# The last expert's rows added on TensorE, and the other experts' rows read back while it runs

## The chip, the cores and the metric
The kernel runs on one core of a Trainium2 chip. The metric is the device time of one execution in microseconds (us). A core has TensorE (PE, matmuls and transposes), VectorE (DVE), ScalarE (ACT), GpSimd (POOL) and SyncE (SP, which here only issues DMAs); each runs its own instruction stream in order, and the streams meet at semaphores. SBUF is the working memory, PSUM (eight banks of 128 x 512 fp32, used here as `PS[:, bank, :]`) is where TensorE writes.

## The reference
Two transformer blocks over 512 tokens of width 1024. The first ends in a mixture of 32 experts, which is where the change is:

```
weights = p_g[:, None] * top_p          # two experts per token, each with a weight
yr = (silu(xb @ w_gate[e]) * (xb @ w_up[e])) @ w_down[e]       # per block of 128 rows
out = segment_sum(yr * row_w[:, None], row_tok)                # the two rows of a token are added
x = x + g2 * moe(h);  return rms_norm(x, final_g)              # end of block one
```

The second block starts with `h = rmsnorm(x)` and `z = h @ w_in`, a matrix of 28 weight units of 1 MB.

## The kernel before
All matmuls are done as three products of split numbers (`mm3`: high x high, high x low, low x high). So every 1 MB weight unit is loaded by SP into one of the buffers `raw[0..7]`, rounded by ACT into `whi` (`act_high`, L1206), and the rest is taken by DVE into `wlo` (`dve_low`, L1875; its event is `lo_v`). Three `whi`/`wlo` pairs form a ring. SP's loads are one list in fixed order (`LOADS`, issued by `sync_load`, L2984): a load waits until the unit that was in its `raw` buffer has been split. For the experts eight buffers rotate; from `w_in2` on, only `raw[0]` and `raw[1]` do.

An expert has six units: two for gate, two for up, two for down. `pe_experts`, `act_experts`, `dve_experts` and `pool_experts` write the order out by hand for each engine, with expert b + 1's first units interleaved with expert b's last. POOL gathers the 128 token rows of expert b + 2 with an indirect DMA (`xg`, L2849), TensorE transposes them (L847), and after the down projection ACT writes the product, scaled by the row's weight, to `yo` (L1472). POOL scatters `yo` to DRAM rows of `y_scratch` (L2841), an array of 1024 rows: one row per token and choice. Its column 1 of table `TB` has the destination row, column 0 the token, column 2 the weight; unused rows of a block have numbers out of bounds and are skipped. An overflow branch for crowded experts (`over_branch`) is skipped in these runs.

Behind the last expert (b = 31) this happens in order:
- all four engines meet (`moe_done`), and ACT waits until the scatters of experts 30 and 31 have landed;
- ACT issues eight DMAs that read `y_scratch` into `ym` (L1528), then splits the high parts of `w_in2` units 0 and 1;
- DVE takes their low parts, and adds the two choices of each group of 128 tokens (`yN`, L2349);
- TensorE transposes the sums (32 transposes, L947) into all eight banks;
- DVE adds the result to `XT` (L2352, event `x3`), ACT squares it into `yN` (L1534), and TensorE sums the squares over the partitions, once with weights `gf` and once with `ones` (L956, two times eight fp32 matmuls);
- ACT and DVE form the scale (L1537, L2356, L1539) and split the normalised rows into `HH` and `HL`, and TensorE starts on `w_in2` (L542).

## Time and profile before

| | us |
|---|---|
| three runs | 3047.74, 3054.37, 3057.34 (median 3054.37) |
| profiled execution: its own time | 3049.59 |
| its span, and mean granted TensorE clock | 3047.5, 0.971 |
| busy: TensorE | 2842.5 (93%) |
| busy: VectorE | 2259.7 (74%) |
| busy: ScalarE | 1481.1 (49%) |
| busy: GpSimd | 598.7 (20%) |

TensorE is busy for most of the span. The experts take the part from about 475 to 1068 us; the end of block one lies between 1068 and 1108 us, and everything behind it is the second block. The profiled execution is 2.1 us longer than its span, and 4.8 us under the median of the three runs.

### The profile page before, as it was taken

The numbers are of one execution on the slowest core, as the hardware profiler recorded it, in microseconds if no ns is written. First come the engines' busy times: TensorE is split into PE (matmuls) and PEld (weight loads), VectorE is DVE, ScalarE is ACT, GpSimd is POOL, SyncE is SP. The second block draws the span as 40 slices with busy tenths as digits, with TensorE's granted clock in tenths as the row PEclk, the third lists the DMA queues.
The fourth block names the chain that finished last, engine by engine and source line by source line (L and its number), as shares of the span: only waits on it lengthen the run. The fifth ranks groups of instructions, "written<-read, shape, count | busy, mean of one in ns | idle before, by whom it ended". The sixth has DMA issues, their size and how long they took to land.

```text
span 3047.5 us, 37281 instructions
## 1 busy us (share of the span) xinstructions
PE 2842.5 (93%) x13623; PEld 2366.9 (78%) x13623; DVE 2259.7 (74%) x3019; ACT 1481.1 (49%) x1990; POOL 598.7 (20%) x478
## 2 busy tenths in 40 slices
PE   5979987999999979998999989999899989999998
PEld 3657756888888748776777779999899978888887
DVE  6465547888888753887954329999998868888886
ACT  3443235888878733554542433563656623333332
POOL 0200111111111100000000010033233434444442
PEclk7999998999999989999999999999999999999999
DMA  7544636999999733232333334487779999999995
GB/s 298 170 159 156 210 114 235 373 368 369 358 358 354 261 128 122 90 115 83 108 128 132 131 114 172 164 287 289 255 280 324 356 374 358 360 370 364 358 366 185
DMA packets 203692, 746.31 MB, mean 245 GB/s; under 512 B 24816, under 2 KB 78192, under 8 KB 146416
## 3 DMA queue, kind: packets, MB, share of 16 engines
q1 hardware_dynamic: 123568, 492.93, 44.9%
q0 software_dynamic: 56912, 179.26, 16.7%
q10 hardware_dynamic: 23024, 71.67, 6.2%
q8 instruction: 111, 1.82, 0.2%
q14 instruction: 77, 0.63, 0.1%
HBM read 670.80 MB, written 98.11 MB: 252 GB/s over the span
## 4 chain that ended last, share of the span: by engine, by line
PE 51%; DVE 18%; issue 6%; DMA 5%; ACT 3%; ACTq 0%; DVEq 0%; POOL 0%; POOLq 0%
PE PS L542 44%; DVE wlo L1875 4%; DMA gbuf<-in_peer_u_dram,IDX 3%; DVE hf L2625 2%; DVE oh L2611 2%; ACT whi L1206 1%; DVE hf L2637 1%; PE PS L996 1%; PE PS L1008 1%; PE PS L847 1%; ACT HH L1845 1%; PE PS L1130 1%; DVE zo L2381 1%; DVE sS L2664 1%; DVE cand L2579 1%
## 5 line engine op out<-in xcount | busy, mean ns | idle before, releaser
L1875 DVE TENSOR_TENSOR wlo<-raw,whi 128x2048 fp32r<-128x2048 f32 x392 | 894.1, 2288 | 359.4 <-ACT whi L1206 322.8
L1206 ACT ACTIVATE whi<-raw 128x2048 fp32r<-128x2048 f32 x392 | 750.8, 1916 | 363.5 <-PE PS L542 304.5
L542 PE MATMUL PS<-HH,whi 128*128 128x512 f32 (+1 forms) x2056 | 791.4, 385 | 41.5 <-DVE wlo L1875 19.1
L542 PE MATMUL PS<-HH,wlo 128*128 128x512 f32 (+1 forms) x2056 | 755.5, 367 | 0.0
L542 PE MATMUL PS<-HL,whi 128*128 128x512 f32 (+1 forms) x2056 | 753.5, 366 | 0.0
L542 PEld LDWEIGHTS PS<-HH,whi 128*128 128x128 f32 x2056 | 393.3, 191 | 104.0 <-DVE wlo L1875 22.4
L542 PEld LDWEIGHTS PS<-HL,whi 128*128 128x128 f32 x2056 | 393.1, 191 | 46.5 <-issue 7.7
L542 PEld LDWEIGHTS PS<-HH,wlo 128*128 128x128 f32 x2056 | 391.6, 190 | 43.2
L542 PE MATMUL PS<-whi,HH 128*128 128x512 f32 (+1 forms) x896 | 352.4, 393 | 22.1 <-DVE HL L2667 16.8
L542 PE MATMUL PS<-wlo,HH 128*128 128x512 f32 (+1 forms) x896 | 348.0, 388 | 0.0
L542 PE MATMUL PS<-whi,HL 128*128 128x512 f32 (+1 forms) x896 | 347.8, 388 | 0.0
L542 PEld LDWEIGHTS PS<-whi,HH 128*128 128x128 f32 x896 | 169.9, 190 | 66.6 <-issue 29.3
L542 PE MATMUL PS<-whi,xh 128*128 128x512 f32 x512 | 208.8, 408 | 1.5 <-DVE xl L2272 1.5
L542 PE MATMUL PS<-whi,xl 128*128 128x512 f32 x512 | 203.0, 397 | 0.0
L542 PE MATMUL PS<-wlo,xh 128*128 128x512 f32 x512 | 202.8, 396 | 0.0
L542 PEld LDWEIGHTS PS<-whi,HL 128*128 128x128 f32 x896 | 170.2, 190 | 35.1 <-issue 0.7
L542 PEld LDWEIGHTS PS<-wlo,HH 128*128 128x128 f32 x896 | 170.0, 190 | 33.8
L2381 DVE SCALAR_TENSOR_TENSOR zo<-zc,cw,zo 128x512 f32<-128x512 f32 x240 | 163.9, 743 | 0.0
L2841 POOL DMA_INDIRECT y_scratch<-yo,TB x32 | 49.3, 1540 | 503.0 <-PE PS L847 438.6
L1821 ACT ACTIVATE sS<-PS 128x384 f32<-128x384 f32 x128 | 61.6, 482 | 160.1 <-PE PS L542 157.8
L2941 POOL DMA_INDIRECT gbuf<-in_peer_u_dram,IDX x64 | 101.8, 1591 | 187.3 <-DVE dots L2625 153.8
L2941 POOL DMA_INDIRECT gbuf<-in_peer_v_dram,IDX x64 | 111.4, 1741 | 124.9 <-DVE hf L2637 109.9
(415 smaller groups left out, 3912.6 us busy)
## 6 DMA issues: line engine op xcount, KB each, us to landing
raw<-in_moe_dram SPq DMA_DIRECT2D x192, 1024.0 KB, 7.3
raw<-in_u_units_dram SPq DMA_DIRECT2D x64, 1024.0 KB, 6.1
...
```

The lines of the kernel that those rows point to most:

```text
L542: ins = t.matmul(dst, a, b, start=(first and n == 0), stop=(last and n == 2))
L847: ins = t.transpose(m.PS[:, 4 + half, 128 * c:128 * c + 128], m.xg[:, i, 128 * (4 * half + c):128 * (4 * half + c) + 128], m.ident[:, :])
L996: ins = t.matmul(m.PS[:, 6, 128 * c2:T], m.vN2[:, c2, c:c + 128], m.PT[:, c2, 128 * c2:T], start=(c2 == 0), stop=(c2 == NT - 1), skip_grou ...
L1008: pe.inc(t.matmul(m.PS[:, 4 + n % 2, 0:128 * (i + 1)], m.Qa[:, h % 2, 128 * i:128 * i + 128], m.Ka[:, h % 2, 0:128 * (i + 1)], start=True, ...
L1206: a.inc(a.e.activation(m.whi[p % HRING][:, :, :], m.raw[RAW_SLOT[load_of(p)]][:, :, :], ACT.Copy), "hi", p)
L1821: a.inc(s.activation(m.sS[u % 2][:, ci, :], m.PS[:, n % 4, 0:TDN], ACT.Gelu_apprx_tanh), "act", n)
L1875: v.inc(v.e.tensor_tensor(m.wlo[h][:, :, :], m.raw[RAW_SLOT[load_of(p)]][:, :, :], m.whi[h][:, :, :].bitcast(F32), ALU.subtract), "lo_v", p)
L2381: ins = e.scalar_tensor_tensor(out=m.zo[:, k, :], in0=m.zc[:, k % 4, 2 + j:2 + j + T], scalar=m.cw[:, k, j:j + 1], in1=m.zo[:, k, :], op0= ...
L2611: v.inc(v.e.tensor_tensor(m.oh[:, n % 4, :, :, :], bass.AP(m.io128, 0, [[128, 128], [0, 2], [0, 4], [1, 128]]), bass.AP(eT, 4 * q, [[512 i ...
L2625: v.inc(e.tensor_tensor_reduce(m.jk[:, :], m.gbuf[i], m.hN[:, :], 1.0, 0.0, ALU.mult, ALU.add, m.dots[:, s:s + 1]), "dot", s)
L2841: g.dma(g.e.indirect_dma_start(m.y2[:, :], bass.IndirectOffsetOnAxis(ap=m.TB[:, b, 1:2], axis=0), m.yo[:, b % 2, :], None, bounds_check=2 ...
L2941: g.dma(g.e.indirect_dma_start(m.gbuf[i], None, m.I["peer_u"] if n < 128 else m.I["peer_v"], bass.IndirectOffsetOnAxis(ap=m.IDX[:, s:s + 1 ...
```

## The change
Expert 31's outputs no longer go to DRAM. Its rows of `y_scratch` are written with zeros by POOL after expert 0 (`pool_last_zero`: a memset of the buffer `ht`, here named `xlast`, and a scatter), and its token rows are gathered after expert 2 into the same buffer (`pool_last_rows`). SP reads `y_scratch` into `raw[6]`, `raw[7]`, `raw[2]` and `raw[3]` (four loads of 1 MB), behind the loads of `w_in2` units 0 and 1, as soon as the scatters of experts 30 and 29 have landed and the last units in those buffers have been split. DVE adds the two choices in place (`dve_sums`). ACT writes expert 31's scaled product as `yhi`, DVE the rest as `ylo`, and DVE makes `put`, a 128 x 512 matrix with a one where the row's token is the column. TensorE transposes the sums, and adds onto them in PSUM `yhi` and `ylo` times `put` for each of eight banks: 16 matmuls of 128 x 512. Banks are taken in the order 0, 1, 4, 5, 6, 7, 2, 3, since banks 2 and 3 hold expert 31's product. DVE's split of `w_in2` unit 1 goes behind the additions to `XT`.

The core of the diff:

```diff
@@ pe_turn_x
-    pe.wait_ge(o + f"xg{i}", b)
+    last = b == N_EXP - 1
+    pe.wait_ge("xlast") if last else pe.wait_ge(o + f"xg{i}", b)
...
@@ pe_experts
     for i in range(NT):
         pe.wait_ge("summed", i)
-        for kc in range(KC):
-            ins = t.transpose(m.PS[:, kc, 128 * i:128 * i + 128], m.yN[:, i, 128 * kc:128 * kc + 128], m.ident[:, :])
-            if i == NT - 1:
-                pe.inc(ins, "yturn", kc)
+    for kc in YTURN:
+        if kc in (2, 3):
+            pe.wait_ge("ylo", kc - 2)
+        for i in range(NT):
+            t.matmul(m.PS[:, kc, 128 * i:128 * i + 128], m.ym[i][:, 0, 128 * kc:128 * kc + 128], m.ident[:, :],
+                     is_transpose=True, start=(i == 0), stop=False)
+    pe.wait_ge("put")
+    pe.wait_ge("ylo", 1)
+    for kc in YTURN:
+        t.matmul(m.PS[:, kc, :], m.yhi[:, 128 * kc:128 * kc + 128], m.put[:, :], start=False, stop=False)
+        pe.inc(t.matmul(m.PS[:, kc, :], m.ylo[:, 128 * kc:128 * kc + 128], m.put[:, :], start=False, stop=True),
+               "yturn", kc)
...
@@ act_experts
-        act_outputs(a, m, b, 0, False)
+        if b + 1 < N_EXP:
+            act_outputs(a, m, b, 0, False)
...
+    for n in range(2):
+        b = N_EXP - 1
+        a.wait_ge("use_m", b, 4 + n)
+        a.inc(a.e.activation(m.yhi[:, 512 * n:512 * n + 512], m.PS[:, 2 + n, :], ACT.Copy,
+                             scale=m.TB[:, b, 2:3].bitcast(F32)), "yhi", n)
     a.mark("experts_done")
...
     a.wait_all("moe_done")
-    a.wait_ge("y_out0", N_EXP - 2)
-    a.wait_ge("y_out1", N_EXP - 1)
-    for i in range(NT):
-        for half in range(2):
-            a.dma(a.e.dma_start(m.ym[:, i, half, :], m.y2[512 * half + 128 * i:512 * half + 128 * i + 128, :]),
-                  f"ym{i}", half)
     act_high(a, m, FIRST["w_in2"] + 1)
     act_warm(a, m, ACT.Sqrt)
...
@@ dve_experts
+    last = N_EXP - 1
+    v.wait_ge("io512")
+    v.inc(e.tensor_copy(m.warm[:, :], m.TB[:, last, 0:1]), "puttok")
+    v.own()
+    v.inc(e.tensor_scalar(m.put[:, :], m.io512[:, :], m.warm[:, 0:1], None, ALU.is_equal), "put")
+    dve_sums(v, m, False)
+    for n in range(2):
+        v.wait_ge("yhi", n)
+        v.inc(e.scalar_tensor_tensor(out=m.ylo[:, 512 * n:512 * n + 512], in0=m.PS[:, 2 + n, :],
+                                     scalar=m.TB[:, last, 2:3].bitcast(F32),
+                                     in1=m.yhi[:, 512 * n:512 * n + 512].bitcast(F32), op0=ALU.mult,
+                                     op1=ALU.subtract), "ylo", n)
     v.mark("experts_done")
...
     v.wait_all("moe_done")
-    dve_low(v, m, FIRST["w_in2"] + 1)
-    for i in range(NT):
-        v.wait_ge(f"ym{i}", 1)
-        v.inc(e.tensor_tensor(m.yN[:, i, :], m.ym[:, i, 0, :], m.ym[:, i, 1, :], ALU.add), "summed", i)
-    for kc in range(KC):
+    dve_low(v, m, FIRST["w_in2"])
+    for kc in YTURN:
         v.wait_ge("yturn", kc)
         v.inc(e.scalar_tensor_tensor(out=m.XT[:, kc, :], in0=m.PS[:, kc, :], scalar=m.mod[:, 40 + kc:41 + kc],
                                      in1=m.XT[:, kc, :], op0=ALU.mult, op1=ALU.add), "x3", kc)
+    dve_low(v, m, FIRST["w_in2"] + 1)
...
@@ dve_sums (new)
+    for i in range(NT):
+        v.wait_ge(o + f"ym{i}")
+        v.inc(v.e.tensor_tensor(m.ym[i][:, 0, :], m.ym[i][:, 0, :], m.ym[i][:, 1, :], ALU.add), o + "summed", i)
...
@@ pool_last_zero, pool_last_rows (new), pool_experts
+    g.inc(g.e.memset(m.xlast, 0.0), "yzero")
+    g.own()
+    g.dma(g.e.indirect_dma_start(m.y2[:, :], bass.IndirectOffsetOnAxis(ap=m.TB[:, N_EXP - 1, 1:2], axis=0), m.xlast,
+                                 None, bounds_check=2 * T - 1, oob_is_err=False), "yzero_out")
+
+
+def pool_last_rows(g, m):
+    g.wait_ge("yzero_out")
+    g.dma(g.e.indirect_dma_start(m.xlast, None, m.h2d[:, :],
+                                 bass.IndirectOffsetOnAxis(ap=m.TB[:, N_EXP - 1, 0:1], axis=0),
+                                 bounds_check=T - 1, oob_is_err=False), "xlast")
...
-    for b in range(N_EXP):
+    for b in range(N_EXP - 1):
         pool_expert(g, m, b, False)
+        if b == 0:
+            g.wait_all("route_done")
+            g.inc(e.iota(m.io512[:, :], pattern=[[1, T]], base=0, channel_multiplier=0,
+                         allow_small_or_imprecise_dtypes=True), "io512")
+            pool_last_zero(g, m)
+        elif b == 2:
+            pool_last_rows(g, m)
...
@@ sync_program
+        if n == LOAD_OF["w_in2", 2]:
+            y.wait_ge("y_out0", N_EXP - 2)
+            y.wait_ge("y_out1", N_EXP - 3)
+            for i in range(NT):
+                y.wait_ge("lo_v", YM_AFTER[i])
+                y.dma(e.dma_start(m.ym[i], y_rows(m, i)), f"ym{i}")
```

Three places of the instruction streams, as the two programs have them. SP's queue around the first `w_in2` loads (`raw_1` is `raw[0]`, `raw_16` and `raw_17` are `raw[6]` and `raw[7]`, `raw_3` and `raw_4` are `raw[2]` and `raw[3]`), before:

```order
L2984 DMA raw_15<-in_moe_dram 128x2048
L2984 DMA raw_1<-in_w_in_dram 128x2048
L2984 DMA raw_2<-in_w_in_dram 128x2048
L2984 DMA raw_1<-in_w_in_dram 128x2048
L2984 DMA raw_2<-in_w_in_dram 128x2048
```

and now:

```order
L3058 DMA raw_15<-in_moe_dram 128x2048
L3058 DMA raw_1<-in_w_in_dram 128x2048
L3058 DMA raw_2<-in_w_in_dram 128x2048
L3091 DMA raw_16<-y_scratch 128x2x1024
L3091 DMA raw_17<-y_scratch 128x2x1024
L3091 DMA raw_3<-y_scratch 128x2x1024
L3091 DMA raw_4<-y_scratch 128x2x1024
L3058 DMA raw_1<-in_w_in_dram 128x2048
```

The four reads stand between units 1 and 2 of `w_in2`. DVE at the end of the experts, before, from the last expert's `hl` to the additions to `XT` (what is skipped belongs to the overflow branch):

```order
L2297 TENSOR_TENSOR hl<-PS,hh 128x512
L3051 TENSOR_LOAD n_over
L3052 COMPARE_AND_BRANCH
...
L1875 TENSOR_TENSOR wlo_8<-raw_1,whi_5 128x2048
L1875 TENSOR_TENSOR wlo_9<-raw_2,whi_6 128x2048
L2349 TENSOR_TENSOR yN<-ym 128x1024 x4
L2352 SCALAR_TENSOR_TENSOR XT<-PS,mod,XT 128x512 x8
L2356 RECIPROCAL ht<-ht 128x512
```

and now:

```order
L2318 TENSOR_TENSOR hl<-PS,hh 128x512
L2368 CAST warm<-TB 128x1
L2370 TENSOR_SCALAR put<-io_125,warm 128x512
L2340 TENSOR_TENSOR raw_16<-raw_16 128x1024
L2340 TENSOR_TENSOR raw_17<-raw_17 128x1024
L2340 TENSOR_TENSOR raw_3<-raw_3 128x1024
L2340 TENSOR_TENSOR raw_4<-raw_4 128x1024
L2374 SCALAR_TENSOR_TENSOR ylo<-PS,TB,yhi 128x512 x2
...
L1896 TENSOR_TENSOR wlo_8<-raw_1,whi_5 128x2048
L2391 SCALAR_TENSOR_TENSOR XT<-PS,mod,XT 128x512 x8
L1896 TENSOR_TENSOR wlo_9<-raw_2,whi_6 128x2048
```

The sums and `ylo` stand ahead of the meeting of the engines, and one of the two splits behind the additions to `XT`. POOL around experts 0 to 2, before:

```order
L2849 DMA xg<-h_scratch,TB 128x1024 x3
L2841 DMA y_scratch<-yo,TB 1024x1024
L2849 DMA xg<-h_scratch,TB 128x1024
L2841 DMA y_scratch<-yo,TB 1024x1024
L2849 DMA xg<-h_scratch,TB 128x1024
L2841 DMA y_scratch<-yo,TB 1024x1024
```

and now:

```order
L2889 DMA xg<-h_scratch,TB 128x1024 x3
L2881 DMA y_scratch<-yo,TB 1024x1024
L2930 IOTA io_125 128x512
L2909 MEMSET ht 128x1024
L2911 DMA y_scratch<-ht,TB 1024x1024
L2889 DMA xg<-h_scratch,TB 128x1024
L2881 DMA y_scratch<-yo,TB 1024x1024
L2889 DMA xg<-h_scratch,TB 128x1024
L2881 DMA y_scratch<-yo,TB 1024x1024
L2917 DMA ht<-h_scratch,TB 128x1024
```

The gather of expert 3's rows, the fourth `xg`, now stands behind an iota, a memset and the scatter of zeros.

## Rows read from the trace of the kernel before

**Rows 1.** Timeline behind the last expert: start, length (us), engine, instruction, [idle before].
```profile
1068.22 0.69 ACT L1472 ACTIVATE yo<-PS,TB 128x512 f32<-128x512 f32 x1 [2.13 <-PE PS L542]
...
1072.43 4.62 ACTq L1528 DMA_DIRECT2D ym<-y_scratch  x8
1077.10 3.71 ACT L1206 ACTIVATE whi<-raw 128x2048 fp32r<-128x2048 f32 x2 [8.19 <-issue]
...
1080.88 1.28 ACT L1238 ACT_TABLE_LOAD   x1
...
1084.82 5.66 PE L947 MATMUL PS<-ident,yN 128*128 128x128 f32 x32 [16.70 <-DVE yN L2349]
1087.93 1.22 DVE L2349 TENSOR_TENSOR yN<-ym 128x1024 f32<-128x1024 f32 x1 [0.90 <-DMA ym<-y_scratch]
1089.84 5.36 DVE L2352 SCALAR_TENSOR_TENSOR XT<-PS,mod,XT 128x512 f32<-128x512 f32 x8 [0.68 <-PE PS L947]
...
1107.61 0.47 PE L542 MATMUL PS<-HH,whi 128*128 128x512 f32 x1 [2.25 <-DVE HL L1926]
```

**Rows 2.** Chain of waits that ended last: start, length (us), what.
```profile
1060.05 8.09 PE PS L542 x24
...
1069.67 2.65 DMA y_scratch<-yo,TB
...
1073.77 7.44 DMA ym<-y_scratch
...
1091.39 13.98 PE PS L956 x32
...
1205.52 2.77 PE PS L542 x12
```

**Rows 3.** The instructions on `y_scratch` between 1045 and 1060 us, with time to landing.
```profile
L2841 POOL DMA_INDIRECT y_scratch<-yo,TB x1: 1562/1562/1562, 1051.3 to 1051.3; - x1
...
DMA to landing us min/median/max: 6.6/6.6/6.6
```

**Rows 4.** The instructions on `y_scratch` between 1000 and 1045 us.
```profile
DMA to landing us min/median/max: 8.4/8.8/9.1
```

**Rows 5.** Busy time by stretch: each engine's, then granted clock, DMA share, GB/s.
```profile
1068.00:1072.00 4.00, 0.12 (x1) 0.00 (x0) 0.00 (x0) 0.69 (x1) 0.98 (x1) 0.97 0.05 11
1072.00:1076.00 4.00, 0.00 (x0) 0.00 (x0) 0.00 (x0) 0.00 (x0) 0.00 (x0) 0.50 0.60 213
1076.00:1080.00 4.00, 0.00 (x0) 0.00 (x0) 0.86 (x1) 2.90 (x2) 0.00 (x0) 0.50 0.98 358
1080.00:1084.00 4.00, 0.00 (x0) 0.00 (x0) 4.00 (x3) 2.29 (x3) 0.00 (x0) 0.50 1.02 416
...
1086.00:1088.00 2.00, 2.00 (x11) 2.00 (x10) 1.10 (x2) 0.00 (x0) 0.00 (x0) 0.50 0.98 414
1088.00:1090.00 2.00, 2.00 (x17) 2.00 (x16) 1.32 (x2) 0.00 (x0) 0.00 (x0) 0.79 0.76 320
```

**Rows 6.** Timeline of the last DVE splits and of the last expert's `hl`.
```profile
1043.99 4.63 DVE L1875 TENSOR_TENSOR wlo<-raw,whi 128x2048 fp32r<-128x2048 f32 x2 [0.75 <-ACT whi L1206]
...
1059.21 0.69 DVE L2297 TENSOR_TENSOR hl<-PS,hh 128x512 fp32r<-128x512 f32 x1 [1.58 <-ACT hh L1463]
```

**Rows 7.** Timeline of POOL and of TensorE's transposes around experts 0 and 1.
```profile
436.47 1.80 POOL L2822 MEMSET xg<- 128x2048 f32 x1
...
509.70 1.03 POOL L2849 DMA_INDIRECT xg<-h_scratch,TB  x1 [0.30 <-issue]
...
524.17 1.04 PE L847 MATMUL PS<-ident,xg 128*128 128x128 f32 x8
```

**Rows 8.** The instructions on `xg`, whole span: time to landing.
```profile
DMA to landing us min/median/max: 3.7/8.2/11.5
```

**Rows 9.** Busy time by stretch: start of the second block.
```profile
1109.00:1112.00 3.00, 2.94 (x8) 1.69 (x9) 3.00 (x6) 1.26 (x2) 0.00 (x0) 0.56 0.00 0
...
1140.00:1160.00 20.00, 20.00 (x90) 16.57 (x89) 9.28 (x9) 8.89 (x10) 0.00 (x0) 1.00 0.34 108
```

More of the change, by code:

```diff
@@ L446, in __init__ @@
             self.yo = sb(st, "yo", [128, 2, 1024])
+            self.xlast = self.ht[:, :, :].rearrange("p a n -> p (a n)")
+            self.yhi, self.ylo = (sb(st, name, [128, 1024], F32R) for name in ("yhi", "ylo"))
+            self.io512, self.put = sb(st, "io512", [128, T]), sb(st, "put", [128, T], F32R)
             self.oraw = self.raw[RING:RING + 2]
@@ L449, in __init__ @@
         with ExitStack() as st:
-            self.ym = sb(st, "ym", [128, NT, 2, 1024])
             self.yN = sb(st, "yN", [128, 4, 1024])
         both.close()
+        self.ym = [t[:, :, :].rearrange("p (k a) n -> p k (a n)", k=2) for t in self.raw[6:8] + self.raw[2:4]]
         with ExitStack() as st:
@@ L847, in pe_turn_x @@
             ins = t.transpose(m.PS[:, 4 + half, 128 * c:128 * c + 128],
-                              m.xg[:, i, 128 * (4 * half + c):128 * (4 * half + c) + 128], m.ident[:, :])
+                              (m.xlast if last else m.xg[:, i, :])[:, 512 * half + 128 * c:512 * half + 128 * c + 128],
+                              m.ident[:, :])
         pe.inc(ins, o + "xturn", b, half)
@@ L912, in pe_overflow @@
         pe.inc(ins, "ouse_m", b, 4 + n)
+YTURN = (0, 1, 4, 5, 6, 7, 2, 3)
 def pe_experts(pe, m):
@@ L945, in pe_experts @@
         pe.wait_ge("summed", i)
-        for kc in range(KC):
-            ins = t.transpose(m.PS[:, kc, 128 * i:128 * i + 128], m.yN[:, i, 128 * kc:128 * kc + 128], m.ident[:, :])
-            if i == NT - 1:
-                pe.inc(ins, "yturn", kc)
+    for kc in YTURN:
[10 more added lines that the diff above has]
+               "yturn", kc)
     pe.wait_ge("gf")
     for r in (3, 2):
-        for kc in range(KC):
+        for n, kc in enumerate(YTURN):
             pe.wait_ge("sq", 2, kc)
@@ L956, in pe_experts @@
             pe.inc(t.matmul(m.PS[:, 3 - r, :], m.gf[:, kc, :] if r == 3 else m.ones[:, :],
-                            m.yN[:, kc // 2, 512 * (kc % 2):512 * (kc % 2) + 512], start=(kc == 0),
-                            stop=(kc == KC - 1)), "ssq", r, kc)
+                            m.yN[:, kc // 2, 512 * (kc % 2):512 * (kc % 2) + 512], start=(n == 0),
+                            stop=(n == KC - 1)), "ssq", r, n)
     pe.mark("norm_done")
@@ L1523, in act_experts @@
     a.wait_all("moe_done")
-    a.wait_ge("y_out0", N_EXP - 2)
-    a.wait_ge("y_out1", N_EXP - 1)
-    for i in range(NT):
-        for half in range(2):
-            a.dma(a.e.dma_start(m.ym[:, i, half, :], m.y2[512 * half + 128 * i:512 * half + 128 * i + 128, :]),
-                  f"ym{i}", half)
     act_high(a, m, FIRST["w_in2"] + 1)
     act_warm(a, m, ACT.Sqrt)
-    for kc in range(KC):
+    for kc in YTURN:
         a.wait_ge("x3", kc)
@@ L2311, in dve_overflow, with dve_sums @@
         next(low)
+def dve_sums(v, m, over):
+    o = "o" * over
+    for i in range(NT):
+        v.wait_ge(o + f"ym{i}")
+        v.inc(v.e.tensor_tensor(m.ym[i][:, 0, :], m.ym[i][:, 0, :], m.ym[i][:, 1, :], ALU.add), o + "summed", i)
 def dve_experts(v, m):
@@ L2342, in dve_experts @@
             dve_overflow(v, m, b)
+        dve_sums(v, m, True)
     m.last_split = N_SOLID - 1
@@ L2345, in dve_experts @@
     v.wait_all("moe_done")
-    dve_low(v, m, FIRST["w_in2"] + 1)
-    for i in range(NT):
-        v.wait_ge(f"ym{i}", 1)
-        v.inc(e.tensor_tensor(m.yN[:, i, :], m.ym[:, i, 0, :], m.ym[:, i, 1, :], ALU.add), "summed", i)
-    for kc in range(KC):
+    dve_low(v, m, FIRST["w_in2"])
+    for kc in YTURN:
         v.wait_ge("yturn", kc)
@@ L2835, in pool_expert @@
 def pool_expert(g, m, b, over):
-    o, last = "o" * over, N_BLK if over else N_EXP
+    o, last = "o" * over, N_BLK if over else N_EXP - 1
     if b + 2 < last:
@@ L2882, in pool_experts @@
         g.wait_ge("oy_out1", N_BLK - 2)
+        for i in range(NT):
+            g.dma(e.dma_start(m.ym[i], y_rows(m, i)), f"oym{i}")
         g.inc(e.memset(m.yo[:, :, 0:1], 0.0), "oclear")
@@ L2964, in pool_peer, with y_rows @@
                 pool_rows(g, m, step)
+def y_rows(m, i):
+    return bass.AP(m.y2, 128 * i * D, [[D, 128], [T * D, 2], [1, D]])
+YM_AFTER = [max(PLACE_OF[kind, i] for n, (kind, i) in enumerate(LOADS)
+                 if RAW_SLOT[n] == k and kind == "moe") for k in (6, 7, 2, 3)]
 def sync_load(y, m, n):
@@ L3011, in sync_program @@
     for n in range(1, done):
+        if n == LOAD_OF["w_in2", 2]:
+            y.wait_ge("y_out0", N_EXP - 2)
+            y.wait_ge("y_out1", N_EXP - 3)
+            for i in range(NT):
+                y.wait_ge("lo_v", YM_AFTER[i])
+                y.dma(e.dma_start(m.ym[i], y_rows(m, i)), f"ym{i}")
         sync_load(y, m, n)
@@ L3053, in over_branch @@
             q.wait_all("experts_done")
-            q.wait_ge("y_out0", N_EXP - 2)
-            q.wait_ge("y_out1", N_EXP - 1)
+            for i in range(NT):
+                q.wait_ge(f"ym{i}")
             yield
```

4 lines of the change are left out of this document (3 added, 1 removed).

## The prediction
> **What bounds the kernel now.** I read the page first: TensorE is busy 93% of the span, so time is to be had where it stands still. The timeline behind the last expert shows one such place. TensorE's last product there ends at 1068.14 us (1060.05 + 8.09) [rows 2] and its next work, the 32 transposes of the sums, starts at 1084.82, an idle time of 16.70 [rows 1]. The chain of waits names what fills it: the scatter of expert 31 lands at 1072.3 (2.65 us), then the read of `y_scratch`, whose chained piece takes 7.44, and behind it DVE's splits and sums [rows 1, 2]. Then come 5.66 us of transposes, the additions to `XT`, and 13.98 us of fp32 matmuls for the sums of squares, which end at 1105.4 [rows 1, 2]. `w_in2` starts at 1107.61 [rows 1]. The windows give the rate of the reads and TensorE's clock: the granted clock was 0.97 on average from 1068 to 1072, 0.50 (the 1.2 GHz level) from 1072 on, and rose again between 1088 and 1090, while transposes ran [rows 5].
>
> **When the sums are there now.** SP can issue the four reads when expert 30's scatter has landed: issued at 1051.3, landing 6.6 us later [rows 3], so 1057.9. The buffers are free long before: the split of the last unit in them ends with the pair at 1043.99 + 4.63 [rows 6]. How long do 4.19 MB take alone? Before, the reads started at 1072.43 [rows 1] and the windows up to 1084 moved 0.85 + 1.43 + 1.66 = 3.95 MB (rate times length) [rows 5]; the remaining 0.24 MB at 416 GB/s take 0.6 us. That is 12.2 us from the first issue. So the last read lands at 1070.2, and DVE's last sum of 1.22 us [rows 1] ends at 1071.5. Bounds: at 416 GB/s all the way behind a start of 1.5 us, 11.6 us; as it really went, beside two loads of weights, the last sum started at 1087.93, thus 15.5 us after the first issue [rows 1]. I take 12.2, since no other load runs then: units 0 and 1 are ahead of the reads in SP's queue, and unit 2 stands behind them. Unit 2 wants unit 0 split first, which will be later than the reads are issued, so it loses nothing.
>
> A page of the Trainium skill, "DMA: Bandwidth & Descriptors", section "Anatomy of one DMA — SWDGE (gpsimd) path", fits a transfer as 2.0 us plus bytes over 436 GB/s, for GpSimd's queue. By that 4.19 MB would take 11.6 us, the end would come 0.6 us earlier, and the rows of this trace, with 416 GB/s in the best window, nearly bear it out.
>
> **TensorE from 1068.1 on.** It waits for all four sums, until 1071.5, instead of 1084.8 for the first. The transposes: at the half clock 11 began in 2 us [rows 5], 0.18 each; at full clock eight take 1.04 us with a tail [rows 7], about 0.12 each. Before, the clock fell 3.9 us behind the last product [rows 2, 5], and at 1109 it was down although TensorE had begun again at 1107.61 [rows 1, 9]. I therefore take it down from 1072 to 1075.5: 22 transposes in 4 us, ten more in 1.2, end 1076.7. The sixteen new matmuls of 128 x 512 have no row; the nearest is the product of the same form, twelve in 2.77 us at full clock, 0.23 each [rows 2], so 3.7 us, end 1080.4. At the half clock all the way they would take twice as much, 7.4; below 3.7 I see no reason to go. What they need is ready: `yhi` is the old `yo` copy of 0.69 us, ended at 1068.9 [rows 1]; `ylo`, two operations like `hl` of 0.69 [rows 6], ends at 1073.0 behind the sums; banks 2 and 3 come last. `put` and its cast fall in DVE's idle time from 1059.9 [rows 6]; of them I know no duration, but anything up to some 5 us is covered, and beyond that they would delay the sums.
>
> **The chain beside it.** The engines meet when `ylo` is done, 1073.0. ACT's two splits (3.71 for both [rows 1]) give unit 0's high part at 1075.0, DVE's low part of 2.3 us (4.63 for two) [rows 6] ends at 1077.4, and the first bank is ready at 1077.2. So the additions to `XT` run 1077.4 to 1082.8 (5.36 [rows 1]). ACT's table load of 1.28 ends at 1078.4, its first square at 1079.1. TensorE is free only at 1080.4, so this chain is just covered, with 1.3 us to spare. The sums of squares then run 13.98 us [rows 2] to 1094.4, no longer fed by anything slower: before they took 0.87 per bank twice, against 0.67 per addition. The deferred split of unit 1 fits in DVE's wait for the first root, as 7 us pass from 1080.4 to there.
>
> **The sum.** 1105.4 - 1094.4 = 11.0 us. Of it 13.3 come from the earlier sums (1084.8 to 1071.5), 3.7 are spent on the new matmuls, and 1.4 come back since the old start of the squares also lay 0.9 behind the transposes and the transposes now run 0.5 shorter. What follows in the second block hangs on this point: TensorE is busy for the whole of 20 us from 1140 on [rows 9], and nothing there waits for an absolute time. So all of it should reach the end.
>
> **Earlier costs.** POOL's iota, memset and scatter of zeros delay the gather of expert 3's rows, issued at 509.70 and used by TensorE at 524.17 [rows 7]. A memset of twice the size took 1.80 us [rows 7], so 0.9; a scatter takes 1.56 [rows 3]; the iota has no row near its size, and I bound it by the larger memset, 0 to 1.8. Together with gaps that is 3 to 5 us. Landing took 8.2 at the median and 11.5 at most [rows 8]: the gather issued at 513.5 lands at 521.7, at worst at 525 to 526. I take nothing, with 2 us as the far end. The gather of expert 31's rows adds some 1.3 us in POOL's idle time, and the bytes are those of before at another time. ACT loses eight DMA issues (4.62 us [rows 1]), in a stretch where it now waits anyway.
>
> Against the profiled execution's own 3049.6 this gives 3038.6. That execution lies 4.8 under the median 3054.4 of the runs shown, which themselves spread over 9.6 us. From the median I get **3043.4 us**, 0.36% less. A change of 0.3%, 9.2 us, is about what a measurement of this kernel tells from none, so the forecast lies near that line.
>
> **Rivals.**
> - *The clock stays up, or the reads are quicker.* With a gap of only 3.4 us TensorE may not be throttled: 32 transposes in 3.8 us and the matmuls end at 1079.0; the squares then start at 1079.2 and 12.2 us are gained. With the reads at their fast bound it is 12.8. For it: 0.97 was granted from 1068 to 1072 [rows 5]. Against it: the drop at 1109 behind a shorter gap. Time 3042.
> - *The clock does not come back for the transposes.* If transposes did not count as work, all 32 would run at 0.18 (5.7 us), and eight of the matmuls at half clock as well: end 1082.5, gain 8.9, time 3045.5. Against it stands the window 1088 to 1090, in which the clock rose with nothing but transposes running [rows 5]. The Trainium skill, "TensorE: Matmul & The Clock Gate", section "Part 4: PE-mode transpose", says that full clock doesn't engage for transpose-mode; this trace disagrees, with 0.79 granted in that window. By the page this case would be the likeliest.
> - *The reads start or end late.* Expert 30's scatter lands in 8.4 to 9.1 us as in the steady state [rows 4], or the reads take the 15.5 us of before. Each us is lost in full: 1.8 to 3.3 us, gain 6 to 9, time 3047. Against it: the 6.6 us was measured under the same load of unit 1.
> - *A part is given back later*, in that the second block's start meets `w_in2` units or splits that are late, 3 to 6 us. Against: unit 2 can be loaded from 1077.4, and TensorE takes up `w_in2` at about 1096.6, with units 0 and 1 first. Time 3048.
> - *Slower: the norm runs at half clock.* If the clock once down stays down through the sparse start, 16 matmuls take 7.4 and the squares 28.0 instead of 14.0: transposes end at 1077.2, all ends at 1112.6, 7.2 us later than before, 3061.6; it decides once the granted clock is still 0.5 behind 1084. With a late gather for expert 3 on top (2 us) it reaches 0.3%. Against it: the clock came back within 5 us of steady work at 1084.8 [rows 5].
>
> **How the numbers follow.** Forecast 0.52, clock up or quick reads 0.18, transposes don't count 0.09, late reads 0.11, given back later 0.06, slower 0.04. Over 9.2 us lie about 0.46 of the forecast's share (11.0 with 1.5 for the clock's phase and 2 or 3 for the runs' own spread), 0.16 of the second and 0.04 of the third: faster 0.66. Slower by over 0.3%: 0.04 with noise. The rest, 0.30, is within. The range reaches from 3036 (14 us gained and a low median) to 3051 (late reads, a high one).
>
> **What would show it.** In the profile after: the last of the four reads lands near 1070, in the sums' wait on a DMA; TensorE idle some 3.4 us instead of 16.7 behind the last expert; 32 transposes and 16 matmuls within 9 us; granted clock 0.5 for about 3.5 us from 1072; the squares at 1080, ended at 1094.4; `w_in2` at 1096.6; TensorE not idle at 524. It is wrong if the reads land after 1073, if TensorE waits at the squares for ACT, or if the stretch from the first `w_in2` product to the end grows.

## The result, and the profile after

| | before | after |
|---|---|---|
| median of the runs of this comparison, us | 3052.68 (six runs, 3047.74 to 3059.14) | 3038.68 (six runs, 3029.92 to 3043.45) |
| ratio after to before, with 95% interval | | 0.9962 [0.9948, 0.9977] |
| profiled execution: own time; span; clock | 3049.59; 3047.5; 0.971 | 3037.57; 3035.8; 0.971 |

By the ratio the kernel is faster by 0.38%, 11.6 us of 3052.7, and the whole interval lies under 1. The two medians of the table lie 14.0 us apart, the two spans 11.7. The forecast was 11.0 us, and 3043.4 as a time. But the profile does not show the 11.0 where they were forecast. For every kernel below I cut the span in three: up to the end of TensorE's last product of expert 31, from there to the end of the sums of squares (the **piece**), and from there to the end (the **rest**). Between the two profiled executions the first part differs by 1.5 us, the piece by 8.7 (37.25 before, 28.52 after), the rest by 1.5 (1942.13 and 1940.68).

The timeline of the kernel after, behind the last expert (start, length in us, engine, instruction, idle before), answers to [rows 1]:

```profile
1056.21 2.27 SPq L3091 DMA_DIRECT2D raw<-y_scratch  x4
...
1058.68 0.49 DVE L2370 TENSOR_SCALAR put<-io,warm 128x512 fp32r<-128x512 f32 x1
...
1066.21 0.39 PE L549 MATMUL PS<-wlo,hh 128*128 128x512 f32 x1
...
1069.95 1.23 DVE L2340 TENSOR_TENSOR raw<-raw 128x1024 f32<-128x1024 f32 x1 [2.49 <-DMA raw<-y_scratch]
1071.09 1.40 DVE L2374 SCALAR_TENSOR_TENSOR ylo<-PS,TB,yhi 128x512 fp32r<-128x512 f32 x2
...
1071.32 6.43 PE L962 MATMUL PS<-ident,raw 128*128 128x128 f32 x32 [4.72 <-DVE raw L2340]
1072.58 3.71 ACT L1226 ACTIVATE whi<-raw 128x2048 fp32r<-128x2048 f32 x2 [5.20 <-DVE ylo L2374]
1074.62 2.29 DVE L1896 TENSOR_TENSOR wlo<-raw,whi 128x2048 fp32r<-128x2048 f32 x1 [2.13 <-ACT whi L1226]
...
1078.32 5.36 DVE L2391 SCALAR_TENSOR_TENSOR XT<-PS,mod,XT 128x512 f32<-128x512 f32 x8 [1.41 <-PE PS L968]
...
1079.10 5.30 ACT L1555 ACTIVATE yN<-XT 128x512 f32<-128x512 f32 x8 [1.24 <-DVE XT L2391]
...
1097.37 0.71 PE L549 MATMUL PS<-HH,whi 128*128 128x512 f32 x1 [2.24 <-DVE HL L1947]
```

Its chain of waits (start, length, what) answers to [rows 2]:

```profile
1049.73 6.46 DMA y_scratch<-yo,TB
...
1057.66 12.26 DMA raw<-y_scratch
```

The chain goes through the same kinds of work as before, but the reads are now issued while expert 31 still computes, and expert 31's own scatter is gone from it. TensorE's idle time is 4.72 us where it was 16.70. ACT's first square starts at 1079.10, 0.8 us behind the first addition, and takes 0.66 (5.30 / 8); TensorE comes to it at 1081.23 with no wait. So the meeting of the two chains is as forecast.

The windows of the kernel after, over the same stretch (columns as in [rows 5]: TensorE, its loads, DVE, ACT, POOL busy, granted clock, DMA share, GB/s):

```profile
1056.00:1058.00 2.00, 0.86 (x4) 0.46 (x4) 0.28 (x2) 0.60 (x1) 0.00 (x0) 0.62 0.31 53
1058.00:1062.00 4.00, 3.34 (x8) 2.70 (x9) 1.96 (x4) 0.00 (x0) 0.00 (x0) 0.50 1.02 416
1062.00:1066.00 4.00, 4.00 (x16) 3.16 (x16) 1.55 (x2) 0.69 (x1) 0.00 (x0) 0.84 1.04 421
1066.00:1068.00 2.00, 0.59 (x3) 0.17 (x1) 1.23 (x1) 0.69 (x1) 0.00 (x0) 1.00 0.90 358
1068.00:1070.00 2.00, 0.00 (x0) 0.00 (x0) 0.05 (x1) 0.00 (x0) 0.00 (x0) 1.00 0.11 33
1070.00:1072.00 2.00, 0.68 (x4) 0.71 (x5) 2.00 (x3) 0.00 (x0) 0.00 (x0) 0.53 0.03 8
1072.00:1074.00 2.00, 2.00 (x11) 2.00 (x11) 0.49 (x1) 1.42 (x1) 0.00 (x0) 0.50 0.04 8
1074.00:1076.00 2.00, 2.00 (x11) 2.00 (x10) 1.38 (x1) 2.00 (x2) 0.00 (x0) 0.50 0.00 0
1076.00:1078.00 2.00, 2.00 (x14) 1.96 (x13) 0.91 (x1) 1.78 (x3) 0.00 (x0) 0.76 0.16 20
```

Three things are to be read here. The data of the four reads has moved by 1068 (416 x 4 + 421 x 4 + 358 x 2 makes 4.06 of 4.19 MB, and 0.1 before 1058), at 416 to 421 GB/s; yet the last read lands at 1069.92, nearly 2 us later, with the DMA engines at a tenth. The clock is down to 1.2 GHz (0.50) from about 1070.1 to 1077.0, 6.9 us, and comes back while transposes run. And it had been down once before: from about 1056.5 on, behind a gap of only 2.39 us (TensorE stood still from 1053.77 to 1056.16, then had 0.86 us of transposes), so that the first products of expert 31's down projection ran at 1.2 GHz.

The early costs, in POOL's timeline of the kernel after:

```profile
506.42 1.58 POOL L2881 DMA_INDIRECT y_scratch<-yo,TB  x1 [27.50 <-ACT yo L1492]
508.01 0.60 POOL L2930 IOTA io<- 128x512 f32 x1
508.53 0.97 POOL L2909 MEMSET ht<- 128x1024 f32 x1
510.30 1.47 POOL L2911 DMA_INDIRECT y_scratch<-ht,TB  x1 [0.80 <-POOL ht L2909]
512.08 1.91 POOL L2889 DMA_INDIRECT xg<-h_scratch,TB  x1 [0.31 <-issue]
```

The gather of expert 3's rows is issued 5.66 us behind expert 0's scatter, where it was 1.89 before (509.70 [rows 7] behind a scatter at 507.81). TensorE transposes its rows at 522.75, 16.33 behind that scatter; before it was 524.17 - 507.81 = 16.36. Nothing is lost. Of the two gathers issued from 505 to 530 us the first is the slower one (512.08 + 9.5 = 521.6):

```profile
DMA to landing us min/median/max: 8.4/8.9/9.5
```

In the kernel before, this gather landed 5.6 us after its issue.

### The profile page after: what moved, and what is told of

It is laid out like the page before. It is cut to its first block, busy times and chain, and to the rows that moved or that the text cites. A ratio compares the mean times of both kernels' runs of the same rounds, so it can differ in the third digit from the quotient of the medians.

```text
span 3035.8 us, 37322 instructions
## 1 busy us (share of the span) xinstructions
PE 2851.3 (94%) x13639; PEld 2375.3 (78%) x13639; DVE 2261.9 (75%) x3023; ACT 1483.0 (49%) x1990; POOL 600.4 (20%) x480
## 4 chain that ended last, share of the span: by engine, by line
PE 52%; DVE 17%; issue 7%; DMA 5%; ACT 3%; ACTq 0%; DVEq 0%; POOL 0%; SPq 0%; POOLq 0%
PE PS L549 45%; DVE wlo L1896 3%; DMA gbuf<-in_peer_u_dram,IDX 3%; DVE hf L2665 2%; DVE oh L2651 2%; ACT whi L1226 1%; DVE hf L2677 1%; PE PS L1016 1%; PE PS L1028 1%; PE PS L855 1%; ACT HH L1866 1%; DMA ht<-in_peer_u_dram,IDX 1%; PE PS L1150 1%; DVE cand L2619 1%; DVE cand L2616 1%
```

## The experiments

All kernels are edits of the changed kernel. The time is the median of the runs, with their number. The last product's end, the piece and the rest are from each profiled execution's timeline (us):

| kernel | time (runs) | last product's end | idle behind it | transposes, from first to last | piece | rest |
|---|---|---|---|---|---|---|
| before | 3052.68 (6) | 1068.12 | 16.70 | 5.66 | 37.25 | 1942.13 |
| after | 3038.68 (6) | 1066.60 | 4.72 | 6.43 | 28.52 | 1940.68 |
| a0_again | 3039.58 (7) | 1068.96 | 4.74 | 6.44 | 28.57 | 1940.27 |
| a0_third | 3037.96 (5) | 1068.17 | 6.42 | 5.62 | 29.44 | 1939.99 |
| e1_late_reads | 3051.63 (12) | 1073.10 | 14.77 | 6.47 | 38.63 | 1941.17 |
| e2_splits_first | 3036.58 (1) | 1068.78 | 4.83 | 6.38 | 28.60 | 1937.42 |
| e3_fill | 3035.89 (1) | 1065.10 | filled | 3.66 | 27.31 | 1941.69 |
| e4_free_reads | 3035.74 (1) | 1071.13 | 1.77 | 3.69 | 23.35 | 1939.52 |
| e5_groups | 3038.88 (1) | 1070.81 | 1.17 | 5.71 | 25.85 | 1940.44 |
| e6_groups_ylo | 3038.69 (5) | 1070.50 | 2.71 | 5.38 | 26.16 | 1940.24 |
| e7_x3_first | 3037.22 (5) | 1068.87 | 1.40 | 4.41 | 23.21 | 1944.02 |
| e7_again | 3037.16 (6) | 1067.96 | 1.32 | 4.72 | 23.44 | 1943.40 |
| e8_four_memsets | 3043.93 (1) | 1069.63 | 4.68 | 6.53 | 28.59 | 1943.98 |

After, a0_again and a0_third are one program: its pieces lie within 0.9 us of each other and its rests within 0.7. The last product's end moves by 8 us among these executions, and nearly all of that is there before any instruction that differs: POOL's scatter of expert 0 starts between 504.72 (e3) and 512.79 (e1), and from there to the last product of expert 31 every one of the thirteen takes 560.2 to 560.4 us. So a time from one run, or one profiled span, says little about an edit; the piece does.

**The changed kernel once more, and its reads held back.** `a0_again` has no edit. `e1_late_reads` keeps all of the change but lets SP issue the four reads only when expert 31's last product is done:

```diff
             y.wait_ge("y_out1", N_EXP - 3)
+            y.wait_ge("use_m", N_EXP - 1, 5)
```

> The changed kernel once more, as it is, for the comparisons of this call. Theory A: the whole gain arises between TensorE's last product of expert 31 and its last sum of squares; that piece was 37.2 us before and 28.5 after, so here it is 28.5 again (within 0.5), and the other 3.0 us of the 11.7 us between the two spans (1.5 ahead of that piece, 1.5 behind it) are chance and change from run to run. Ratio to the kernel before 0.996 to 0.998. Rival B: the 3.0 us belong to the change; then the last product of expert 31 again ends at 1066.6 or earlier, and from the last sum of squares to the end it again takes 1940.7 or less.

> SP issues the four reads of y_scratch only when TensorE has ended expert 31's last product; the outputs of expert 31 are still added on TensorE. Theory A (the gain is the reads beside the last expert): the reads take 13.7 us from 1066.6, the last sum ends at 1081.6, and the piece from the last product to the last sum of squares is 28.5 + 10.4 = 38.9 us, 1.7 longer than the 37.2 of before: adding on TensorE by itself costs a little. Ratio to before 1.000 to 1.001. Rival C (the gain is that expert 31's scatter and its landing, 3.5 us, are gone from the chain): the piece is about 34 to 35, and the ratio 0.999.

`a0_again` took 3039.58 us (ratio 0.9967 [0.9954, 0.9979]). Its piece is 28.57 again. Of the 3.0 us outside the piece, the 1.5 ahead of it did not come again (the last product ended at 1068.96), but the rest did (1940.27, and 1939.99 in `a0_third`), so the part of the rival that concerns the rest stands; with one profile of the kernel before it can't be settled. `e1_late_reads` took 3051.63, ratio 1.0008 [0.9999, 1.0017]: without the early reads all of the gain is gone. Its timeline:

```profile
1073.21 2.40 SPq L3092 DMA_DIRECT2D raw<-y_scratch  x4
...
1086.49 1.23 DVE L2340 TENSOR_TENSOR raw<-raw 128x1024 f32<-128x1024 f32 x1 [1.20 <-DMA raw<-y_scratch]
...
1087.87 6.47 PE L962 MATMUL PS<-ident,raw 128*128 128x128 f32 x32 [14.76 <-DVE raw L2340]
```

The piece is 38.63 where 38.9 was expected, and the rival's 34 to 35 is refuted: the reads need 13.3 us from the first issue to the last landing here too (13.7 in the kernel after), so what hides them is only their early start. Beside `a0_again` the early issue is worth 10.1 us of piece and 12.0 of median. Leaving out expert 31's scatter alone buys nothing: the wait is 1.9 us shorter than before, but the transposes take 0.8 longer, and 3.5 us instead of 0.9 pass between them and the squares, most of it in the sixteen matmuls.

**TensorE kept busy through its wait.** `e3_fill` puts twenty products behind the last expert, into a bank that is written anew afterwards:

```diff
     pe.mark("moe_done")
+    for n in range(20):
+        t.matmul(m.PS[:, 0, :], m.hh[:, x, n % 4, :], m.whi[h][:, n % 4, :], start=True, stop=True)
```

> Twenty more products of 128 x 512 into bank 0 behind expert 31's last product, whose result is overwritten: TensorE has something to do while it waits for the sums. Theory A': the clock is then still at full when the transposes start; they take about 3.8 us in place of 6.43, and the piece from the last product of the expert to the last sum of squares falls from 28.5 to 26 (the additions to XT, first at 1076.9 behind the split of w_in2's unit 0, may take back up to 0.5). Rival D: the transposes take 6.4 us for another reason than the clock (their order over banks, or four different source buffers), and the piece stays at 28.5 or grows.

```profile
1066.59 4.93 PE L958 MATMUL PS<-whi,hh 128*128 128x512 f32 x20 [1.49 <-issue]
...
1068.41 1.22 DVE L2343 TENSOR_TENSOR raw<-raw 128x1024 f32<-128x1024 f32 x1 [2.28 <-DMA raw<-y_scratch]
...
1071.36 3.66 PE L965 MATMUL PS<-ident,raw 128*128 128x128 f32 x32
```

The transposes take 3.66 us instead of 6.43, so 2.8 us of the piece are the clock that fell in the wait, and the rival that they are slow for another reason is refuted. The twenty products outlast the last sum (1069.63) by 1.7 us, which is why the piece is 27.31 and not the 25.6 that it would be without them; the one run took 3035.89 us, which can't be told from the kernel after.

**The reads free of the scatters.** `e4_free_reads` reads the token rows instead of `y_scratch`, so that SP waits for no scatter (it leaves out the experts' outputs; POOL takes over the two waits behind its last expert):

```diff
-            y.wait_ge("y_out0", N_EXP - 2)
-            y.wait_ge("y_out1", N_EXP - 3)
...
-                y.dma(e.dma_start(m.ym[i], y_rows(m, i)), f"ym{i}")
+                y.dma(e.dma_start(m.ym[i], bass.AP(m.h2d, 128 * i * D, [[D, 128], [0, 2], [1, D]])), f"ym{i}")
```

> The four reads take the same bytes from another DRAM array (the token rows), so they need not wait for the scatters of experts 29 and 30; the sums are then not those of the reference. Theory A: the reads are issued at about 1050.5, land beside unit 1 of w_in2 by 1066, the sums are done before the last product, TensorE has no gap, the clock stays up, and the piece becomes bound by expert 31's own ylo and the split of w_in2's unit 0: about 22 to 23 us. Rival E: the reads end after the expert in any case, because DMA is full, and the piece stays above 27.

```profile
1055.39 2.47 SPq L3091 DMA_DIRECT2D raw<-h_scratch  x4
...
1071.52 1.23 DVE L2340 TENSOR_TENSOR raw<-raw 128x1024 f32<-128x1024 f32 x1 [1.19 <-DMA raw<-h_scratch]
...
1072.90 3.69 PE L962 MATMUL PS<-ident,raw 128*128 128x128 f32 x32 [1.77 <-DVE raw L2340]
```

The piece is 23.35, near the 22 to 23 expected, but one step of the expectation failed: the wait did not go wholly. They stand behind `w_in2` unit 1 in SP's queue, which waits for its buffer until 1055.02, so they started 15.7 us ahead of the last product's end (1071.13), where it is 10.4 in the kernel after, and with unit 1's load beside them they took 16.1. A wait of 1.77 us is left. A gap of 1.8 us did not bring the clock down for the transposes, one of 4.7 did; for what lies between see `e6_groups_ylo`.

**Both deferred splits done first.** `e2_splits_first` takes the low part of unit 1 at its old place, in front of the additions:

```diff
-    dve_low(v, m, FIRST["w_in2"])
+    dve_low(v, m, FIRST["w_in2"] + 1)
     for kc in YTURN:
```

(and no low part behind them).

> DVE takes the low part of w_in2's unit 1 ahead of the additions to XT again, as before the change. Theory A: that chain has room, since TensorE is the later one; the additions start 0.9 us later (1079.2 in the time of the first trace, in place of 1078.3), the first square is ready at 1080.7, still ahead of TensorE at 1081.2, and the piece from expert 31's last product to the last sum of squares stays at 28.5 (within 0.3). Rival F: moving the split is part of the gain; then the piece grows by the length of the split, 2.3 us, to 30.8.

```profile
1076.91 4.49 DVE L1896 TENSOR_TENSOR wlo<-raw,whi 128x2048 fp32r<-128x2048 f32 x2 [2.12 <-ACT whi L1226]
...
1081.32 5.35 DVE L2391 SCALAR_TENSOR_TENSOR XT<-PS,mod,XT 128x512 f32<-128x512 f32 x8
1082.10 5.30 ACT L1555 ACTIVATE yN<-XT 128x512 f32<-128x512 f32 x8 [1.95 <-DVE XT L2391]
...
1083.49 7.03 PE L976 MATMUL PS<-yN,gf 128*128 128x512 f32 x16
```

The first square starts at 1082.10, is ready 0.66 later, and TensorE comes at 1083.49 without a wait. The piece is 28.60 (28.5 expected, 30.8 by the rival). So the deferred split earns nothing: the side chain has 0.7 us of room even with the split ahead of it, since TensorE is later than forecast.

**Transposes by groups, in the wait.** In the changed kernel TensorE waits for all four sums, so that its transposes end 6.6 us behind the last sum (1077.75 and 1071.18); before, they ran beside the sums and ended 1.3 us behind the last one. `e5_groups` takes six banks of each group as soon as its sum is there:

```diff
-    for i in range(NT):
-        pe.wait_ge("summed", i)
-    for kc in YTURN:
-        ...
+    for i, banks in [(i, YTURN[:6]) for i in range(NT)] + [(i, (2, 3)) for i in range(NT)]:
+        pe.wait_ge("summed", i)
+        for kc in banks:
```

> TensorE transposes each group of 128 tokens when its own sum is ready, for the six free banks, and banks 2 and 3 last; DVE's order is unchanged. Theory A (idle time waiting for all four sums is what is left to win): 18 of the 32 transposes fall in the wait, 14 stay behind the last sum, and the split of w_in2's unit 0 becomes the later chain: piece 26, in place of 28.5. Rival G: the few transposes in the wait don't hold the clock up, and the 14 and the 16 products run at half clock: piece 27.5 to 28.5.

```profile
1071.98 2.19 PE L961 MATMUL PS<-ident,raw 128*128 128x128 f32 x18 [1.17 <-issue]
...
1075.39 0.99 PE L961 MATMUL PS<-ident,raw 128*128 128x128 f32 x7 [1.22 <-DVE raw L2339]
...
1082.69 7.10 PE L975 MATMUL PS<-yN,gf 128*128 128x512 f32 x16 [1.34 <-ACT yN L1554]
```

Eighteen transposes ran within the wait, at the full clock, and the piece came to 25.85 (26 expected). TensorE now waits 1.34 us for ACT at the squares: the splits of `w_in2` unit 0 on ACT and DVE, which come behind `ylo`, have become the longer chain. That is the wait which the prediction had priced as covered by 1.3 us; in the changed kernel it was.

**The side chain shortened too.** `e6_groups_ylo` also takes `ylo` ahead of the last sum, so that 24 transposes can run before it. `e7_x3_first` is `e6_groups_ylo` with DVE's low parts of both units behind the additions, and on ACT the table load first, then unit 0's high part, the squares, and unit 1's high part:

```diff
-    act_high(a, m, FIRST["w_in2"] + 1)
     act_warm(a, m, ACT.Sqrt)
+    act_high(a, m, FIRST["w_in2"])
...
+    act_high(a, m, FIRST["w_in2"] + 1)
...
-    dve_low(v, m, FIRST["w_in2"])
     for kc in YTURN:
```

> As e5_groups, and DVE writes ylo ahead of the last sum, so that banks 2 and 3 can be transposed in the wait too and only 8 transposes stay behind the last sum; the engines meet after the last sum in place of ylo, 1.4 us earlier. Theory A: the first square then waits for ACT's two splits and the table load, at about 1077.2 in the time of the first trace: piece 24.6 with a full clock, 26.9 with a half one. Ratio to before 0.995 to 0.997.

> As e6_groups_ylo, and the additions to XT stand ahead of both splits on DVE, and ACT loads its table first, splits w_in2's unit 0, and takes unit 1 behind the squares. Theory A: nothing but TensorE is left on the path behind the last sum; 8 transposes, 16 products and the squares: piece 23.1 with a full clock, 26.9 with a half one, and 24.5 as a guess between; ratio to before about 0.995. Rival H: the splits, now behind the additions, delay DVE's reciprocal or the loads of w_in2's units 2 and 3, and what the piece gains is lost between the last sum of squares and the first product of w_in2, 2.25 us now, or in the 1941 us behind it.

`e6_groups_ylo`: 3038.69 us, ratio 0.9963 [0.995, 0.9977]. Its piece of 26.16 misses the 24.6 that were expected with a full clock, and is no shorter than that of `e5_groups`. Its timeline:

```profile
1072.94 1.23 DVE L2339 TENSOR_TENSOR raw<-raw 128x1024 f32<-128x1024 f32 x1 [3.88 <-DMA raw<-y_scratch]
1073.21 5.38 PE L961 MATMUL PS<-ident,raw 128*128 128x128 f32 x32 [2.72 <-issue]
```

Its window from 1074 to 1075:

```profile
1074.00:1075.00 1.00, 1.00 (x8) 1.00 (x7) 1.00 (x3) 0.00 (x0) 0.00 (x0) 0.63 0.12 49
```

The third read landed late here, and the gap was 2.7 us. The granted clock was still 1.00 from 1073 to 1074, fell in the next us although transposes were running, and was 0.50 up to 1077. So the length of a gap alone does not tell whether the clock falls. The changed kernel shows the same in front of `w_in2`: behind gaps of 2.25 and 2.24 us the clock fell in the kernel after (0.57 in the first 4 us) and did not fall in `a0_third` (1.00 for 8 us).

`e7_x3_first`: piece 23.21, the low end of what was expected, 3037.22 us, ratio 0.9962 [0.9949, 0.9976]. Its timeline:

```profile
1070.27 2.84 PE L961 MATMUL PS<-ident,raw 128*128 128x128 f32 x24 [1.40 <-DVE raw L2340]
...
1073.59 1.09 PE L961 MATMUL PS<-ident,raw 128*128 128x128 f32 x8 [0.48 <-DVE raw L2340]
...
1078.19 7.03 PE L975 MATMUL PS<-yN,gf 128*128 128x512 f32 x16
```

Transposes at full clock, no wait at the squares, 5.3 us less in the piece, and no gain to be seen in the time, though each of the two ratios is only good to 4 us: the rest is 1944.02.

**Is it given back, or chance?** `e7_again` and `a0_third` are `e7_x3_first` and the changed kernel without an edit, side by side.

> The kernel of e7_x3_first once more. There the piece from expert 31's last product to the last sum of squares was 23.2 us, 5.3 less than in the changed kernel, yet the part behind it took 1944.0 us, more than in any other profile (1937.4 to 1942.1). Theory A (chance): the piece is 23.2 again, the part behind lies within 1937 to 1942, and the ratio to the changed kernel run beside it is 0.998. Rival H (given back): the part behind is 1943 to 1945 again, and the ratio to the changed kernel is 1.000.

> The changed kernel again, beside e7_again on the same chip: piece 28.5, the part behind it 1938 to 1942, ratio to the kernel before 0.996 to 0.998. The two theories on e7 differ in how far e7's time lies below this one: 5 us by chance theory A, nothing by rival H.

`e7_again` took 3037.16 us (3034.95 to 3039.13), ratio 0.9957 [0.9944, 0.9969]; `a0_third` 3037.96 (3036.27 to 3039.38), ratio 0.9959 [0.9945, 0.9972]. The piece of `a0_third` is 29.44 where 28.5 was expected: between its second and third read 5.5 us passed, and the four took 15.3 us. The pieces of the two differ by 6.0 us, the medians by 0.8 (the profiled spans by 2.8), the rests by 3.4 the other way. So the 6.0 do not reach the end, and the long rest of this kernel came twice, so it is hardly chance from run to run. But `e8_four_memsets` below has the instructions of the changed kernel behind the piece, a piece no shorter, and a rest of 1943.98 as well. So a rest of 1944 does not need a shorter piece, and that it is the price of one is not shown. Where does it arise? The windows of the first 52 us behind the first `w_in2` product show one place. The kernel after:

```profile
1097.37:1101.37 4.00, 4.00 (x10) 2.65 (x11) 4.00 (x7) 1.90 (x3) 0.00 (x0) 0.57 0.00 0
1101.37:1105.37 4.00, 4.00 (x19) 3.27 (x19) 3.77 (x7) 1.90 (x3) 0.00 (x0) 1.00 0.01 2
```

`a0_third`, its first 4 us:

```profile
1099.85:1103.85 4.00, 2.99 (x10) 1.66 (x11) 4.00 (x7) 1.89 (x3) 0.00 (x0) 1.00 0.00 0
```

`e7_again`:

```profile
1093.64:1097.64 4.00, 3.52 (x10) 2.01 (x11) 4.00 (x7) 1.89 (x3) 0.00 (x0) 0.73 0.00 0
1097.64:1101.64 4.00, 4.00 (x17) 3.24 (x17) 3.77 (x7) 1.90 (x3) 0.00 (x0) 0.84 0.00 2
```

The first and the last have a dip of the clock there, `a0_third` has none. In the kernel after it falls in the first 4 us, where ten matmuls are all that DVE's `HL` lets through at either level; then nineteen begin in the next 4. In `e7_again` the dip comes later and takes two of these nineteen. POOL's transfer of `c_scratch`, 52 us on, is issued 52.21 us behind the first `w_in2` product in after, 52.22 and 52.24 in its repeats, 52.98 and 52.90 in the two e7 kernels: 0.7 us. So an early dip (0.57, then 1.00) costs no more than none at all. The kernel before has the late dip as well (0.72 and then 0.86), and 52.89; `e4_free_reads` too (0.76 and 0.81), and 53.03. A further 1.7 to 1.8 us are lost up to POOL's first transfer into `sN` (703.79 and 703.69 against 701.25 in after), where the clock of the stretch 1600 to 1700 is 0.93 in both, 0.97 in after; but `a0_third` has 703.22 and 0.95 there as well, so that beside it only 0.5 us are lost up to that point and 2.9 behind it. What lies behind that transfer differs among all kernels by up to 5 us, with no pattern that I can see. So 0.7 us of the longer rest goes, at one place, with the time of the clock's dip, in all thirteen executions; no experiment moved the dip alone. The other 2.7 us I leave open.

**Four more memsets ahead of expert 3's gather.** `e8_four_memsets` does the memset of the zeros five times:

```diff
-    g.inc(g.e.memset(m.xlast, 0.0), "yzero")
+    for n in range(5):
+        g.own()
+        g.inc(g.e.memset(m.xlast, 0.0), "yzero", n)
```

> The changed kernel with POOL's memset of zeros done five times in a row in place of once, 4.1 us more before the scatter of zeros and before the gather of expert 3's rows. In the trace after, that gather was issued 5.66 us behind expert 0's scatter (512.08 and 506.42), took 9.5 us to land (521.6), and TensorE took its rows at 522.75: 1.2 us of room. Theory A: the change's own delay was just covered; with 4.1 more the gather lands at 525.7 and TensorE's transposes of those rows come 19.2 us behind expert 0's scatter, in place of 16.3, so TensorE stands still for some 2.9 us there. Rival I: the gather lands sooner when it is issued later, or TensorE has other work ahead of it, and nothing moves (16.3).

```profile
509.30 1.58 POOL L2881 DMA_INDIRECT y_scratch<-yo,TB  x1 [27.77 <-ACT yo L1492]
...
511.55 5.00 POOL L2911 MEMSET ht<- 128x1024 f32 x5
...
519.96 1.03 POOL L2889 DMA_INDIRECT xg<-h_scratch,TB  x1 [0.30 <-issue]
...
525.69 1.09 PE L855 MATMUL PS<-ident,xg 128*128 128x128 f32 x8
```

Its gathers from 505 to 530 us:

```profile
DMA to landing us min/median/max: 5.7/6.2/6.7
```

The gather is issued 10.66 us behind expert 0's scatter, 5 us later than in the kernel after, and its rows are used 16.39 behind it, the same as ever (16.33, 16.36). I had expected a stall from a landing time of about 9 us; but this gather landed in 5.7 us, the one in the kernel after in 9.5. The rival was right. The landing itself came 1.2 us later behind the scatter than in the kernel after (16.4 and 15.2 us), for an issue 5 us later. TensorE's weight load waited 0.3 us for it, so here the room was just used up. Why it landed faster no run shows. The one run took 3043.93 us: its piece is that of the kernel after (28.59), its rest is 1943.98.

## Why the prediction was right

The mechanism is the one forecast. That the total agrees so well (11.6 by the ratio, 11.7 by the spans, 11.0 forecast) is in part luck: the piece, where all of it was forecast, gave 8.7, and 3 us came from parts for which nothing was forecast. By its steps:

1. **Reads issued 10 us ahead of the last product's end**: 10.2 forecast, 10.4 measured (1056.21 against 1066.60). Right; `e1_late_reads` shows that this one step carries the gain.
2. **Reads take 12.2 us**: mis-sized. They took 13.7, 13.3 in `e1_late_reads`. The working added up data by rate until 4.19 MB were there, and left out the nearly 2 us between the last data and the landing. Its far bound of 15.5 us, seen beside other loads, was nearly reached without any in `a0_third` (15.3). The idle time was 4.72 instead of 3.4: 1.3 us of the gain gone. The sum with "2.0 us plus bytes over 436 GB/s", from "DMA: Bandwidth & Descriptors" of the Trainium skill, section "Anatomy of one DMA — SWDGE (gpsimd) path", was 11.6 and further off; it is meant for one transfer, and four were in a row here.
3. **Transposes 5.2 us, at half clock for 3.5**: mis-sized. 6.43 us. The clock fell 3.5 us behind the last product (at about 1070.1), where 3.9 was forecast, but it stayed down for 6.9 us instead of 3.5. From 1072 to 1076 22 transposes started, as forecast, but the clock was back only behind 1076.9, when most of the 32 had started. 1.2 us gone. `e3_fill` (3.66) and `e4_free_reads` (3.69) show what the clock costs here: 2.8 us.
4. **Sixteen matmuls 3.7 us, covered side chain**: right. 3.64 from 1077.75 to 1081.39. In the whole, transposes' end to squares' start went from 0.91 to 3.48. `put` took 0.49. The first square was ready (1079.76) 1.5 us ahead of TensorE, where 1.3 was forecast; `e5_groups` shows this chain taking over once transposes are done within the wait.
5. **Squares 13.98**: 13.9, right.
6. **POOL's detour costs nothing**: right, though the reason was only half right. The margin was to be 2.5 us on a landing of 8.2; it landed in 9.5 with 1.2 us to spare, and with 5 us more delay in 5.7, with 0.3 us of waiting. From expert 0's scatter to the last product of expert 31 the kernel before takes 560.3 us and the one after 560.2.
7. **Everything behind shifts with it**: the rest was 1.5 us shorter. Up to 52 us behind the first `w_in2` product 0.7 of that is the dip of the clock which fell in a sparse stretch; the other 0.8 stay open, as all three rests of the changed kernel lie under the one of before. The 1.5 us ahead of the piece are no gain of the change: ahead of the changed instructions, where the programs are the same, the executions already lie up to 8 us apart, and `a0_again` and `a0_third` have their last product at 1068.96 and 1068.17, where before has 1068.12.

So the piece gave 8.7: 12.0 from the shorter wait, less 0.8 for slower transposes, less 2.6 for the matmuls, 0.1 from the squares. The 11.6 of the total are 8.7 and 3 us, of which only 0.7 go with something seen in the traces, the place of the dip.

The rivals: the clock did not stay up. With the gap at 4.7 us it fell, with 1.8 us it did not, and in `e6_groups_ylo` 2.7 us were enough; so the 3.4 us of the forecast might not have kept it up either. The late reads came to a part of their price, 1.3 us, for another reason (the landing, not the scatter or other loads); in `a0_third` they came to 3 us (an idle time of 6.42), of which its piece shows only 0.9 beside the kernel after, as the transposes took 0.8 less (5.62). "Part given back later" did not happen to this change; `e7_x3_first` lost part of its gain later, with the cause open. The norm did not run at half clock. On the case that transposes don't count for the clock: the granted clock went from 0.50 to 0.76 between 1076 and 1078, nearly all of it with transposes running, and in `e3_fill`, `e4_free_reads` and the first 24 of `e7_x3_first` each took 0.114 to 0.118 us against the 0.18 at the half clock. The rule of "TensorE: Matmul & The Clock Gate", section "Part 4: PE-mode transpose", in the Trainium skill, is not borne out here, as it was not in [rows 5]. By size, though, the 8.9 of this rival is nearest to the 8.7 of the piece, for a reason that is not its own.
